# The down product of two MLPs by seven block products in place of eight, with GpSimd forming the weight combinations

## What is computed

```python
def sqrelu_mlp(x, w_up, w_down):                       # x 512x1024, w_up 1024x4096, w_down 4096x1024
    return jnp.square(jax.nn.relu(x @ w_up)) @ w_down

def first_block(x, ...):
    for layer in range(2):
        h = attention(x, ...) @ w_out                  # differs by layer
        x = layer_norm(ALPHA * x + h, ...)
        h = sqrelu_mlp(x, mlp_w_up[layer], mlp_w_down[layer])
        x = layer_norm(ALPHA * x + h, ...)
# second_block: six modulation vectors from c (the ada columns, w_ada 1024x6144),
# then a token mixer and a convolutional feed-forward net on x
```

## Time and profile before

| | us |
|---|---|
| runs shown: median (lowest to highest) | 1912.75 (1912.38 to 1912.87) |
| profiled execution, from the first to the last instruction | 1913.1 |
| PE busy | 1859.2 (97%) |
| DVE busy | 1174.5 (61%) |
| ACT busy | 773.4 (40%) |
| POOL busy | 582.9 (30%) |

### The profile page before, as it was taken

One profiled execution on the slowest core, in us unless ns is written; L12 is line 12 of the kernel. 1 busy time (PEld: TensorE's weight loads), 2 busy tenths in 40 slices (PEclk: granted clock), 3 DMA queues, 4 the chain that ended last, 5 costly groups with the idle time before them and its releaser, 6 DMA issues.

```text
span 1913.1 us, 25510 instructions
## 1 busy us (share of the span) xinstructions
PE 1859.2 (97%) x9628; PEld 1519.7 (79%) x9628; DVE 1174.5 (61%) x2001; ACT 773.4 (40%) x1320; POOL 582.9 (30%) x442
## 2 busy tenths in 40 slices
PE   9999899999999999998999999999999999999997
PEld 7876568788888888866888888889887788888876
DVE  4568857742573542176775257555559788676766
ACT  4246643321332242385342133327445554434342
POOL 1234533100000010183210000115346557676740
PEclk9999999999999999999999999999999999999999
DMA  7321033643453132302255245421211323333344
GB/s 278 120 93 45 1 132 111 224 151 109 135 185 121 67 110 95 104 2 89 89 198 176 91 152 176 159 88 67 88 45 67 110 89 110 115 121 117 112 153 154
DMA packets 39392, 222.29 MB, mean 116 GB/s; under 512 B 5936, under 2 KB 6256, under 8 KB 18928
## 3 DMA queue, kind: packets, MB, share of 16 engines
q1 hardware_dynamic: 27616, 178.94, 26.2%
q0 software_dynamic: 11664, 41.80, 6.7%
HBM read 216.59 MB, written 2.10 MB: 114 GB/s over the span
## 4 chain that ended last, share of the span: by engine, by line
PE 78%; DVE 13%; DMA 3%; ACT 2%; POOL 2%; issue 2%; SPq 0%; POOLq 0%; ACTq 0%; DVEq 0%
PE G L421 35%; PE G L2674 7%; PE G L2560 5%; PE TR L2674 5%; PE OB L2674 5%; PE G L2581 4%; PE TR L421 2%; DMA KS_sb<-ada 2%; PE OB L421 2%; PE G L1717 2%; POOL weights_low L460 1%; PE TR L2560 1%; DVE weights_low L460 1%; PE OB L1717 1%; PE TR L1717 1%
## 5 line engine op out<-in xcount | busy, mean ns | idle before, releaser
L460 DVE TENSOR_TENSOR weights_low<-ring_sb,weights_high 128x1024 fp32r<-128x1024 f32 x206 | 255.8, 1246 | 377.4 <-ACT weights_high L454 377.3
L454 ACT ACTIVATE weights_high<-ring_sb 128x1024 fp32r<-128x1024 f32 (+1 forms) x308 | 316.2, 1032 | 398.6 <-PE OB L2674 131.3
L421 PE MATMUL G<-xt_high,weights_high 128*128 128x512 f32 (+1 forms) x1224 | 451.3, 369 | 2.3 <-issue 1.5
L421 PE MATMUL G<-xt_low,weights_high 128*128 128x512 f32 (+1 forms) x1224 | 449.0, 367 | 0.0
L421 PE MATMUL G<-xt_high,weights_low 128*128 128x512 f32 (+1 forms) x1224 | 448.9, 367 | 0.0
L460 POOL TENSOR_TENSOR weights_low<-ring_sb,weights_high 128x1024 fp32r<-128x1024 f32 (+2 forms) x102 | 245.5, 2418 | 306.7 <-ACT weights_high L454 306.7
L421 PEld LDWEIGHTS G<-xt_high,weights_high 128*128 128x128 f32 x1224 | 228.4, 187 | 43.1 <-issue 3.6
L421 PEld LDWEIGHTS G<-xt_high,weights_low 128*128 128x128 f32 x1224 | 228.4, 187 | 38.6
L421 PEld LDWEIGHTS G<-xt_low,weights_high 128*128 128x128 f32 x1224 | 228.4, 187 | 37.6
L2435 POOL DMA_DIRECT2D KS_sb<-ada x64 | 34.0, 531 | 472.2 <-DVE og_sb L3040 472.2
L2274 DVE SCALAR_TENSOR_TENSOR KS_sb<-G,cols_sb,KS_sb 128x441 f32<-128x441 f32 (+2 forms) x160 | 109.9, 687 | 65.1 <-ACT KS_sb L1991 65.1
(11 more groups left out here) (576 smaller groups left out, 3657.4 us busy)
## 6 DMA issues: line engine op xcount, KB each, us to landing
ring_sb<-chunks SPq DMA_DIRECT2D x155, 1024.0 KB, 4.9
KS_sb<-ada POOLq DMA_DIRECT2D x64, 512.0 KB, 4.7
wide_sb<-x_features SPq DMA_DIRECT2D x4, 512.0 KB, 9.2
X_sb<-slabs SPq DMA_DIRECT2D x1, 2048.0 KB, 13.9
ring_sb<-slabs SPq DMA_DIRECT2D x1, 2048.0 KB, 7.7
rows_sb<-ln_gain POOLq DMA_DIRECT2D x4, 512.0 KB, 5.1
rows_sb<-ln_bias POOLq DMA_DIRECT2D x4, 512.0 KB, 6.0
X_sb<-x SPq DMA_DIRECT2D x4, 512.0 KB, 8.8
```

Of the source, the lines that this page charges most:

```text
L421: mm = nc.tensor.matmul(out, lhsT=a, rhs=b, start=(3 * i + j == 0), stop=(3 * i + j == n - 1))
L454: nc.scalar.activation(quarter_part(weights(stage, n)[0], stage, n), quarter_part(raw_quarter(Q), stage, n), ACT.Copy).then_inc(w_hi, 1)
L460: tt_(out=quarter_part(wl, stage, n), in0=quarter_part(raw_quarter(Q), stage, n), in1=quarter_part(wh, stage, n), op=ALU.subtract).then_in ...
```

## The change

The hidden features are paired: unit u (u = 0 to 15) holds hidden chunks 2u and 2u+1, and the down product is taken as a product of 2x2 blocks: token halves of 256 by hidden chunk (even, odd), and hidden chunk by column halves of 512. It is made by seven block products instead of eight (Winograd's form of Strassen's algorithm). Each block product is 2 token tiles by 16 units by 3 matmuls.

- **Two plain products** (`plain_blocks`) use the hidden chunks and weights as they are, first token half by first column half. Unit u of both is 12 matmuls and stands behind up 2u+5, so ups and plain products alternate: two ups, one unit.
- **Five products of sums**: POOL forms four combinations of each unit's weights in place (`weight_sums`, 4 operations of 128x512), stores them to a DRAM tensor `down_sums` (1 MB a unit), and forms four combinations of the hidden blocks in place (`hidden_sums`, 4 of 128x256). SyncE (SP) reads the weight combinations back. Kind B (two products, 12 matmuls a unit) follows the plain ones; kinds E and F (three products, 12 and 6 matmuls a unit) come last; POOL makes one more hidden sum a unit for them. F of units 10 to 15 is held back to the very end.
- **Splitting the hidden blocks**: relu and square now write float32 into `wide`; ACT and DVE split each block when it is used (`block_high`, `block_low`).
- **Evacuation**: each of the seven products goes from its PSUM banks into up to four blocks of `X` (`evacuate`), and the layer norm of all four tiles follows the end of kind E (tiles 0 and 1) and of kind F (tiles 2 and 3).
- **ada**: the loads go to SP's queue, and the steps on DVE are spread over ups 1 to 29 (`ADA_STEPS`); `mlp1` moves the context's norm and transposes, and `w_in` takes its products in another order.

```diff
+    LINEAR = [("U", c) for c in range(6)]
+    for c in range(6, UPS, 2):
+        LINEAR += [("D", (c - 6) // 2), ("U", c), ("U", c + 1)]
+    LINEAR += [("D", u) for u in range(13, UNITS)] + [("B", u) for u in range(UNITS)] + [(x, u) for u in range(UNITS) for x in "EF"]
...
+    ADA_STEPS = {1: (0, (0,)), 2: (0, (1, 2)), 3: (0, (3, 4, 5)), 4: (0, (6, 7)), 6: (1, (0, 1, 2)), 7: (1, (3, 4, 5)), 8: (1, (6, 7)),
...
-            gp.wait_ge(even_scored, 8 * N_EVEN)
-            ada_loads((0, 1))
...
+                def weight_sums(u):
+                    n, x = 4 * (UNITS * i + u), raw_down(u)
+                    b11, b21, b12, b22 = (x[:, c:c + 512] for c in (0, 512, 1024, 1536))
+                    gp.wait_ge(down_in[down_slot(u)], down_count(stage, u))
+                    tt(out=b22, in0=b22, in1=b12, op=ALU.subtract).then_inc(raw_sums, 1)
+                    gp.wait_ge(raw_sums, n + 1)
+                    tt(out=b12, in0=b12, in1=b11, op=ALU.subtract).then_inc(raw_sums, 1)
+                    gp.wait_ge(w_lo, SPLIT0[stage] + AT["D", u] + 1)
+                    gp.wait_ge(raw_sums, n + 2)
+                    tt(out=b11, in0=b22, in1=b11, op=ALU.add).then_inc(raw_sums, 1)
+                    gp.wait_ge(raw_sums, n + 3)
+                    tt(out=b21, in0=b11, in1=b21, op=ALU.subtract).then_inc(raw_sums, 1)
+                    gp.wait_ge(raw_sums, n + 4)
+                    gp.dma_start(A["down_sums"][i, u], x).then_inc(sums_stored[down_slot(u)], 16)
+
+                def hidden_sums(u):
+                    n = 4 * (UNITS * i + u)
+                    a11, a21 = hid(2 * u)[:, 0:256], hid(2 * u)[:, 256:512]
+                    a12, a22 = hid(2 * u + 1)[:, 0:256], hid(2 * u + 1)[:, 256:512]
+                    gp.wait_ge(staged_l, staged_at(stage, "0", u))
+                    tt(out=a22, in0=a21, in1=a22, op=ALU.add).then_inc(hid_sums, 1)
+                    gp.wait_ge(hid_sums, n + 1)
+                    tt(out=a21, in0=a11, in1=a21, op=ALU.subtract).then_inc(hid_sums, 1)
+                    gp.wait_ge(hid_sums, n + 2)
+                    tt(out=a11, in0=a22, in1=a11, op=ALU.subtract).then_inc(hid_sums, 1)
+                    gp.wait_ge(hid_sums, n + 3)
+                    tt(out=a12, in0=a12, in1=a11, op=ALU.subtract).then_inc(hid_sums, 1)
...
+                def evacuate(t, half, bank, first=False, sign=ALU.add):
+
+                    x = X[:, t, half * 512:(half + 1) * 512]
+                    if first:
+                        ins = nc.vector.scalar_tensor_tensor(out=x, in0=x, scalar=alpha, in1=bank[:, :], op0=ALU.mult, op1=ALU.add)
+                    else:
+                        ins = nc.vector.tensor_tensor(out=x, in0=x, in1=bank[:, :], op=sign)
+                    ins.then_inc(dve_out, 1)
...
+                def down(u):
+                    if u == 0:
+                        sp.wait_ge(w_lo, Q + 4)
...
+                    else:
+                        sp.wait_ge(sums_stored[u % 2], down_count(stage, u - 2))
+                    sp.dma_start(raw_down(u), A["downs"][i, u]).then_inc(down_in[down_slot(u)], 16)
...
+                for c in range(4, UPS):
+                    up(c)
+                    if c % 2 and c > 4:
+                        plain_blocks((c - 5) // 2)
+                for u in (UNITS - 2, UNITS - 1):
+                    plain_blocks(u)
...
+                fourth(HELD, (0, 1))
+                fourth(HELD + 1, (0, 1)).then_inc(quarters, 2)
+                for u in range(HELD + 2, UNITS):
+                    mm = fourth(u, (0,))
+                mm.then_inc(prod_done, 1)
+                for u in range(HELD + 2, UNITS):
+                    mm = fourth(u, (1,))
+                    if u == HELD + 3:
+                        turn_first()
+                mm.then_inc(quarters, 4)
+                turn_second()
```

More of the change, by code:

```diff
@@ L137, in build @@
     st.add("x1", tr=8)
-    st.add("mlp0", quarters=64, act=32, hidden=32, dve=16, ln=28, std=4)
+    st.add("mlp0", quarters=96, act=32, dve=28, ln=28, std=4)
     st.add("x2", tr=8)
@@ L144, in build @@
     st.add("x_ctx", tr=4)
-    st.add("mlp1", quarters=64, act=32, hidden=32, dve=16, ln=52, std=8, norm=4)
+    st.add("mlp1", quarters=96, act=32, dve=28, ln=52, std=8, norm=4)
     st.add("x4", tr=8)
@@ L197, in build @@
         at, tiles_at = at + n, tiles_at + n_tiles
+    RAW0 = {stage: n - MLP_QUARTERS * sum(SPLIT0[m] < n for m in MLPS) for stage, n in SPLIT0.items()}
     FORGET = 1
@@ L480, in n_quarters, with hid, hid_r, flat @@
         def n_quarters(stage):
-            return len(FFN) if stage == "ffn2" else sum(a + b for a, b in PARTS[stage])
+            return len(FFN)
+        def hid(c):
+            return wide[:, c, :]
+        def hid_r(c):
+            return (Hh, Hl)[c // 16][:, c % 16, :]
+        def flat(x):
+            return x.rearrange("p a b -> p (a b)")
+        def quarters_in(eng, stage, n):
+            eng.wait_ge(quarters, st(stage, "quarters") + n)
+        def both(a, u, c):
+            return a[:, 2 * u % a.shape[1]:2 * u % a.shape[1] + 2, c:c + 256]
@@ new lines, in block_low, with raw_down @@
+        def block_low(dve, stage, x, u):
+            dve.wait_ge(staged_h, staged_at(stage, x, u))
+            hi, lo = staged_pair(x, u)
+            if x == "A":
+                src = hid(2 * u)[:, 256:512]
+            else:
+                src, hi = both(wide, u, 256 if x == "B" else 0), pair_of(hi)
+                if x != "E":
+                    lo = pair_of(lo)
+            nc.vector.tensor_tensor(out=lo, in0=src, in1=hi, op=ALU.subtract).then_inc(staged_l, 1)
+        def raw_down(u):
+            return flat(KS4[:, :, :]) if u == UNITS - 1 else flat(rows[:, :, :]) if u % 2 else ring[:, 1, 2048:4096]
@@ L2443, in _, with block_sums @@
-            gp.wait_ge(even_scored, 8 * N_EVEN)
-            ada_loads((0, 1))
-            gp.wait_ge(hidden, st("mlp0", "hidden") + 32)
+            def block_sums(stage, gain):
+                tt, i = nc.gpsimd.tensor_tensor, MLPS.index(stage)
+                def weight_sums(u):
[24 more added lines that the diff above has]
+                    tt(out=a12, in0=a12, in1=a11, op=ALU.subtract).then_inc(hid_sums, 1)
+                for u in range(UNITS):
+                    weight_sums(u)
+                    hidden_sums(u)
+                if stage == "mlp1":
+                    gp.wait_ge(sums_stored[2], down_count(stage, UNITS - 1))
+                    gp.dma_start(ctok, A["ctx_2"].rearrange("o (t p) d -> p (o t) d", p=P)).then_inc(s_ctx, 16)
+                    gpsimd_inputs(gp)
+                gain()
+                for u in range(UNITS):
+                    gp.wait_ge(staged_l, staged_at(stage, "B", u))
+                    a11, a21 = hid(2 * u)[:, 0:256], hid(2 * u)[:, 256:512]
+                    tt(out=a21, in0=a11, in1=a21, op=ALU.add).then_inc(hid_last, 1)
```

716 lines of the change are left out of this document (485 added, 231 removed), and 3 rows, old and new, of the table ADA_STEPS.

## The result

| | before | after |
|---|---|---|
| runs shown: median (lowest to highest), us | 1912.81 (1912.38 to 1913.15) | 1953.89 (1949.77 to 1957.37) |
| profiled execution, first to last instruction, us | 1913.1 | 1950.6 |

The change makes the kernel slower: the ratio is 1.0203, with a 95% interval of 1.0176 to 1.023. The prediction had 1903.5 in a range of 1884 to 1930. 41 us are lost where 9 were to be won.

What follows compares the result with a forecast made beforehand. PE's own work was taken to bound the MLP stages. The terms -43.5 + 3 + 10 + 11.8 + 7.5 + 2 gave -9.2 us: 1903.9 on the profiled execution, 1903.5 as median, range 1884 to 1930.

Steps and rivals of the forecast that it cites:

- 192 matmuls: Down products on PE: 96 fewer matmuls an MLP, 192 in all at 0.2267 us each, -43.5 us.
- idle beside the ups: Ups and plain units: DVE needs 13.9 us of 13.6 a unit; 1.5 an MLP, +3, bounds 0 and 32.
- idle in kind B: Kind B: DVE's 58 us against PE's 43.5 and a lead of about 5; 5 an MLP taken, +10.
- idle in the tails: Stage ends, where PE waits for all four tiles' norms on DVE: +11.8 in mlp0, +7.5 in mlp1.
- matmuls at a lower clock: Behind the two tails: a few microseconds of matmuls at half pace, +2 us (0 to 6).
- the lead of three split quarters: Beside the ups: a lead of about 11 us absorbs most of DVE's lateness, some 4 us over 14 units.
- The ledger of DVE's work: Beside the ups: DVE's own 7.1 us plus 6.8 of delay by POOL, 13.9 against PE's 13.6 a unit.
- Costed at nothing: the ada loads: SP's queue behind the ups: DVE needs a slice every 4 us or so, 1 MB lands in 4.9; no cost.
- Rival A: Beside the ups: POOL blocks DVE for its full time, 15.3 us a unit; +32, about 1933; chance 0.22.
- Rival B: Ups and kind B cost nothing as ada steps and sums fall into gaps; about 1881; chance 0.24.
- rival C: SP's queue: loads wait for stores, so PE waits for ups; about 1930 and above; chance 0.06.
- The prediction's last sentence: Wrong altogether if the clock falls in the MLPs' short waits, making every matmul term too small; no row prices it.

Runs made afterwards that it cites:

- the small sums: The changed kernel with POOL's weight sums and hidden sums on 8 columns in place of 512 and 256: 1902.6 us, ratio 0.9946.
- The best full one: The changed kernel with ada sums and turn later, POOL's last sums, second-block inputs and context work in kind E, mlp1's tail reordered: 1921.45 us, ratio 1.0031.
- the last run: The rearranged kernel (ratio 1.0031) with POOL's sums on 8 columns in place of 512 and 256: 1901.6 us, ratio 0.9943.
- small weight sums: The changed kernel with only POOL's weight sums on 8 columns, hidden sums whole: 1912.1 us, ratio 0.9986.

## Why the prediction was wrong

Step by step, on the profiled executions:

| step | predicted, us | after, us |
|---|---|---|
| 192 matmuls | -43.5 | -43.5 (count 9628 to 9436) |
| idle beside the ups | +3 | 23.0, less 2.1 before |
| idle in kind B | +10 | 13.8 |
| idle in the tails | +19.3 | 8.4 + 12.1, less 1.5 before |
| matmuls at a lower clock | +2 | 27 in all longer matmuls, about 24 by the clock |

The rows of idle make 53.7 of the 54.0. Two terms were missed, by 18 and by 25 us, and those are nearly the whole error: 1903.9 on the profiled execution, 18, 25 and 4 for kind B make 1950.9, against 1950.6.

**The ups: the step that failed** is "most of it inside the lead of three split quarters". The ledger of DVE's work against 13.6 us a unit was, if anything, too high: by the small sums POOL costs a step 0.52, half a first step 0.3, a low 0.2 in the mean and a block low 0.2, or 3.5 x 0.52 + 0.3 + 3 x 0.2 + 0.2 = 2.9 a unit and not 6.8. But the lead is one of weight lows, and PE asks DVE for something else too, which has no lead: the ada sum, behind a given up, needs the eighth step of its job. "Costed at nothing: the ada loads" weighed them the same way, as a rate (a slice every 4 us, landed in 4.9), and not by the time at which PE needs the last step. In the wait seen close the last two steps began at 367.80, when PE was at the last matmul ahead of the sum. Moving six of these sums by one up took 27 us of the 41 back; taking away the loads gave 29, taking away POOL's sums 51, kind B's waits among them.

**Rival A** had the idle beside the ups (over 20; 23.0 found) and not the way: DVE was to be over nine tenths busy from 330 to 560; it was at 70% there, and PE waited at L2890, not at a weight low. Rival B and rival C didn't occur: no wait of PE in the ups ends on SP's queue, and the stores landed in 5.7 to 6.7 us in the median. The DMA's 4 MB a unit were added up wrongly: two ups of 512 KB, a down unit and its store are 3, and only with two slices of `w_ada` 4; the share of three quarters came true (0.77).

**The rule that spoke against the change.** The Trainium skill, "SBUF — State Buffer", section "Who interferes with whom", has the one that comes first hold the shared pair for its whole instruction and the other blocked. The runs agree that there is such contention between DVE's two-input operations and POOL's (0.75 to 1.27 a step, gone with the sums). As a price it was too high where the two alternate; in the row of ten sums it was too low, since DVE was kept out for all ten and not for one.

Not all of DVE's work is held up: beside nine sums in kind B of `mlp0`, block lows took 1.23 for 0.68, while DVE's evacuations, which have one input in PSUM, took 0.64 to 0.68.

**The clock.** "A few microseconds of matmuls at half pace give +2" counted the two tails. The waits in the ups and kind B were there as well, and in or behind the waits of 3.2 to 9.0 us there the granted clock was 0.5 for 3.4 to 10.2 us. The prediction's last sentence names this case as the one that no row prices. About 24 of the 27 us are the clock by the estimate above; what the rest is stays open. The small sums bear it out: there PE was busy at the lower level for 39.7 us in place of 70.1, half of the difference is 15, and its busy time fell by 18. With the later ada sums it fell by only 3, but that profile is of the slowest of four runs, with 10 us more at the lower level ahead of the first MLP.

**Kind B and the tails.** Kind B has 3.0 and 10.8 where 5 and 5 were forecast, the second by the row of ten sums. The tails were right in their sum (19.3 forecast, 19.0 found), and that is partly luck. `mlp0` has 8.4 for 11.8, with the three pieces forecast (4.6, 1.5 and 2.3 for 4.3, 2.5 and 5). `mlp1` has 10.6 more than before, for 7.5: 5.9 stands at tile 0 (4.1 forecast), and 6.2 are a wait for POOL's lows of `w_in` that the prediction doesn't have.

What stays open: no order that was tried gets below the kernel before. The best full one is at 1.0031 of it, and of its 51 us over the time before less 43.5, 20 are POOL's sums by the last run; the rest is the tails, the clock and kind E, which weren't tried apart.

## What to carry to other kernels

A step that a second engine makes beside the main work must be costed at the place where the first engine asks for it, not as a share of an engine's time: list every semaphore that the bound engine waits for in the stage, also those of side work, and how far ahead of each its producer runs. Where a change makes all of a side job later by a microsecond or two, look first at the numbers that place its consumers. And an idle stretch of a few microseconds on TensorE is to be priced with the matmuls behind it, which ran at half pace here.

## What the runs showed of the hardware

- One DVE operation with two SBUF inputs (0.68 us alone) took 7.59 beside ten GpSimd operations in a row, which ran at 0.68 each, though by the profile it began 0.20 before the first of them; with small weight sums it took 7.58, the same way. In kind B of `mlp0` nine such sums took 10.70 and alternated with DVE's. Which of the two comes about was not tried apart.
- At waits of 3.31 and 8.97 us the granted clock of TensorE was at its lower level for 3.4 and 10.2 us, 4.8 of the second still inside the wait, and the matmuls of 512 columns behind them started 0.43 apart in place of 0.23.
